# TensorE's eight chunks of a recurrence written out one by one, in place of a loop on registers

## The reference: what is computed

```python
def step(S, inp):
    rt, wt, kt, vt, at, bt = inp
    S = (S * wt[:, :, None, :]
         + jnp.einsum('bhij,bhj->bhi', S, at)[..., None] * bt[:, :, None, :]
         + vt[..., None] * kt[:, :, None, :])
    return S, jnp.einsum('bhij,bhj->bhi', S, rt)
S_fin, y = lax.scan(step, S0, (r, w, k, v, -kk, kk * a))
```

## Time and profile before

| what | value |
|---|---|
| three runs | 4151.55, 4153.0, 4154.53 us; median 4153.0 |
| profiled execution | 4150.38 us, its span 4148.7 us |
| mean granted TensorE clock in the span | 0.941 of full speed |
| TensorE busy with matmuls | 3701.4 us (89%) |
| VectorE, ScalarE, GpSimd busy | 1607.5, 958.5, 53.6 us |
| moved by DMA | 496.8 MB, 119 GB/s from and to HBM over the span |

### The profile page before, as it was taken

How to read it: one execution, slowest core, us unless ns; L and a number is a source line. 1 busy time by engine, 2 the same in 40 slices (tenths; PEclk the granted TensorE clock), 3 DMA queues, 4 the chain that set the end, 5 groups by cost and what they waited for, 6 DMA issues and landing times. The chain is left out here.

```text
span 4148.7 us, 76893 instructions
## 1 busy us (share of the span) xinstructions
PE 3701.4 (89%) x32597; PEld 3463.7 (83%) x32597; DVE 1607.5 (39%) x2336; ACT 958.5 (23%) x1142; POOL 53.6 (1%) x72
## 2 busy tenths in 40 slices
PE   8998997766188987889998699999999999999998
PEld 7998994533188877779995299999999999999997
DVE  3223435502766654332322123333433343344334
ACT  3111112302233333221312113221121112112112
POOL 0000000000001000000000000000000000000000
PEclk9999998966599999999999799999999999999999
DMA  4322228987100004732123622222222222222222
GB/s 156 114 104 92 91 83 351 402 351 287 41 1 0 0 14 152 266 120 91 71 91 132 264 91 71 92 92 92 92 92 91 86 93 89 92 92 92 89 95 72
DMA packets 102399, 496.80 MB, mean 120 GB/s; under 512 B 13121, under 2 KB 19522, under 8 KB 66114
## 3 DMA queue, kind: packets, MB, share of 16 engines
q1 hardware_dynamic: 97538, 476.93, 30.7%
q0 software_dynamic: 4672, 17.01, 1.1%
HBM read 472.32 MB, written 21.58 MB: 119 GB/s over the span
## 5 line engine op out<-in xcount | busy, mean ns | idle before, releaser
L1953 PE MATMUL ps<-hf_hi,whi_f 128*128 128x260 f32 x2816 | 568.3, 283 | 19.3 <-DVE x L1943 9.4
L1953 PE MATMUL ps<-hf_hi,wlo_f 128*128 128x260 f32 x2816 | 567.9, 283 | 0.0
L1953 PE MATMUL ps<-hf_lo,whi_f 128*128 128x260 f32 x2816 | 567.0, 283 | 0.0
L184 ACT ACTIVATE whi_f<-raw 128x2048 fp32r<-128x2048 f32 x132 | 252.8, 1915 | 970.2 <-PE ps L1953 947.9
L1953 PEld LDWEIGHTS ps<-hf_hi,whi_f 128*128 128x128 f32 x2816 | 434.8, 189 | 21.2 <-DVE x L1943 10.6
L1953 PEld LDWEIGHTS ps<-hf_hi,wlo_f 128*128 128x128 f32 x2816 | 434.6, 189 | 0.0
L1953 PEld LDWEIGHTS ps<-hf_lo,whi_f 128*128 128x128 f32 x2816 | 433.5, 188 | 0.0
L188 DVE TENSOR_TENSOR wlo_f<-raw,whi_f 128x2048 fp32r<-128x2048 f32 x132 | 302.6, 2293 | 146.9 <-ACT whi_f L184 146.9
L222 PE MATMUL ps<-h_hi,whi_a 128*128 128x260 f32 x1600 | 324.2, 284 | 29.0 <-DVE h_lo L267 17.8
L222 PE MATMUL ps<-h_hi,wlo_a 128*128 128x260 f32 x1600 | 324.0, 284 | 0.0
L222 PE MATMUL ps<-h_lo,whi_a 128*128 128x260 f32 x1600 | 323.6, 284 | 0.0
(11 more groups left out here) (367 smaller groups left out, 5473.2 us busy)
## 6 DMA issues: line engine op xcount, KB each, us to landing
raw<-w SPq DMA_DIRECT2D x262, 1024.0 KB, 4.8
page_ring<-kc SPq DMA_DIRECT2D x128, 512.0 KB, 6.2
page_ring<-vc SPq DMA_DIRECT2D x128, 512.0 KB, 6.1
mem_ring<-mkc SPq DMA_DIRECT2D x8, 2048.0 KB, 17.2
mem_ring<-mvc SPq DMA_DIRECT2D x8, 2048.0 KB, 17.2
qkv<-ev_a POOLq DMA_DIRECT2D x24, 260.0 KB, 2.3
qkv_head<-qkv SPq DMA_DIRECT2D x8, 780.0 KB, 6.8
rkv<-xt SPq DMA_DIRECT2D x4, 1040.0 KB, 8.4
```

Source lines behind the costliest of these rows:

```text
L184: act.activation(whi[:, u, :], raw[:, u, :], ACT.Copy).then_inc(whi_done, 1)
L1953: mm = pe.matmul(ps[:, 2 * u + s, 0:m], wt[:, wslot, kcol:kcol + 128], t[:, k, a:a + m], start=(first and wt is whi and t is th), stop=(la ...
```

## The change

TensorE no longer uses `turns_of` in the recurrence. Its body is called eight times with a Python number, so that all eight chunks stand one behind the other in its program and each wait compares with a constant. The products, their order and every other engine's program stay as they are.

```diff
--- before.py
+++ after.py
@@ -1383,7 +1383,8 @@
                         pe.wait_ge(W0.sem, W0.at("u3b"))
                         for q in range(2):
                             grams(q)
-                        turns_of(pe, body)
+                        for c in range(NCH):
+                            body(c, c == NCH - 1)
 
                 wkv_out = sem("wkv_out")
                 with nc.Block() as block:
```

## The result

The changed kernel takes 4175.4 us (median of five runs, 4173.95 to 4178.98) against 4153.0 us, a ratio of 1.0057 with a 95% interval from 1.0042 to 1.0071: slower by 22 us. The forecast was 4187 us, slower. The profiled execution took 4178.98 us, its span 4177.3 us, 28.6 over the span before; so the profile shown here is of a run at the slow end of the five, and the differences read from it are a little larger than that of the medians.

The account below looks back on a forecast made before the run. The prediction took TensorE to bound the kernel, busy 3701 of 4148.7 us. Eight feed-forward returns at 2.7 + 1.7 us, less 1 us, gave +34 us on 4153.0: 4187 us, own range 4159 to 4205, overall range 4148 to 4203.

Parts of the forecast that it names:

- The recurrence, waits and return: In the recurrence, constant waits and no loop return on TensorE: -1 us together, between 0 and -2.1.
- The 21 blocks more: Unrolled recurrence: its 21 extra instruction blocks are fetched ahead in straight code and cost nothing.
- The shift, 148 instructions: Feed-forward loop: 5524 added instructions, 21 x 256 + 148, move its target 148 toward its block's end.
- The place: Feed-forward loop's target: 157 instructions left in its block before, give or take 5, and 9 after.
- The second pause: After each feed-forward return TensorE waits for a second block: 2.7 us extra idle, 1.0 to 3.1.
- The clock: After each feed-forward return TensorE's clock may fall to half rate: 1.7 us lost, between nothing and 3.4.
- The sum: Eight feed-forward returns at 2.7 + 1.7 us make 35 us, less 1 us: +34 us, from +6 to +52.
- (1): Rival: the feed-forward loop's target isn't near its block's end, so no second miss: 4152 us, chance 0.30.
- (2): Rival: the recurrence's six returns each load their target as the feed-forward's do; unrolling saves 9 us: 4144, chance 0.02.
- (3): Rival: small shifts change which recurrence chunks fall where in the clock's pattern, faster or slower: 4147 to 4157, chance 0.09.
- (4): Rival: the recurrence's straight code isn't fetched in time, 1 us at each of 21 blocks: 4174 us, chance 0.03.

Follow-up runs that it names:

- runs 5: TensorE's eleven feed-forward turns written out in place of their loop, on the kernel before (4132.9 us) and on the changed kernel (4132.7 us).
- N = 160: The kernel before with 160 unused semaphore increments on TensorE's queue in the sample's step, ahead of the feed-forward loop: ratio 1.0086.
- N = 176: The kernel before with 176 unused semaphore increments on TensorE's queue in the sample's step, ahead of the feed-forward loop: ratio 1.0003.
- run 1: The changed kernel with 108 unused semaphore increments on TensorE's queue, restoring the feed-forward loop's place in its block: 4155.2 us, ratio 1.0009.
- run 3: The kernel before with 256 unused semaphore increments, one whole block, on TensorE's queue in the sample's step: 4150.5 us, ratio 0.9996.
- N = 148: The kernel before with 148 unused semaphore increments on TensorE's queue, moving the feed-forward loop as the change does: 4178.3 us, ratio 1.0062.
- N = 132: The kernel before with 132 unused semaphore increments on TensorE's queue in the sample's step, ahead of the feed-forward loop: ratio 1.0017.

## Why the prediction was right

- **The recurrence, waits and return: -1 us, between 0 and -2.1.** Right within what can be seen. The list of waits kept its four rows, and runs 5 put the change's own worth at 0 us (4132.7 against 4132.9), with an uncertainty of some 6 us on either. So -1 us can't be told from nothing.
- **The 21 blocks more at nothing.** Right: no "issue" in the recurrence, and in runs 5 more than 70 blocks at the full pace of matmuls without a pause.
- **The shift, 148 instructions.** Right: 148 increments on the kernel before gave the changed kernel's turns to 0.1 us, 108 on the changed kernel undid them.
- **The place: 157 left before, 9 after.** Off by 11, outside my 5. The matmuls that ran, nine where I had three or four, show 168 and 20. The step that failed is the distance between sequencer and array. I took the 20 records that were to come when the *target's* packet started, and used them for a packet asked for at a block's entry. A branch spends more time ahead of its packet. The window of the kernel before from the branch to the start of the packet, the stretch ahead of the earlier trace rows:

```profile
2994.10:2995.04 0.94, 0.94 (x10) 0.94 (x10) 0.08 (x1) 0.00 (x0) 0.00 (x0) 1.00 0.00 0
```

  So 40 records were to come at the branch and 20 when its packet started. If a packet at a block's entry starts 0.7 us behind its request, as it does behind the return, only 11 records pass, the sequencer is 29 ahead, and 137 + 29 + 2 = 168. This was worked out after the fact and not tested by itself.
- **The second pause: 2.7 us a return, 1.0 to 3.1.** Measured 1.6 to 2.0, 1.8 in the mean. The time until the block comes was right (2.9 to 3.3 us from restart to restart, where I had 3.2); what was mis-sized is the work in hand, 1.3 us for nine matmuls and not 0.4.
- **The clock: 1.7 us a return.** Near: a stretch of 3.4 us at 0.50 at each return, of which some 0.45 us still fall in the pause in the return shown, so that matmuls lose 1.5 us; this is what the second pause of 1.8 leaves of the 3.3 us by which a turn grew. That the clock would fall was argued, from a pause longer than 1.5 us; the size was only the middle of two bounds, and its coming out is luck.
- **The sum.** 8 x 3.3 = 26 us in the profiled execution, 22 in the medians, against 34. Nearly all of the difference lies in the place: N = 160, with 8 instructions left where I had thought of 9, comes to 4.5 us a return and 37 us in the medians, where I had 4.4 and 35.
- **The rivals.** (1) is what happens with N = 176. It was farther than I thought: not ten instructions but more than 20 were needed to carry the target across. (2) is false for the recurrence and true for the feed-forward loop, as runs 5 show. The Trainium skill's rule ("Runtime: NRT & Kernel Launch", "Instruction fetch mechanics"), that a taken branch to code not held waits for a fetch and that kernels should therefore be unrolled where they can, holds for the feed-forward loop, where writing out gained 18 us; for the recurrence, whose returns took 0.21 us, it gained nothing. (3) stays open in size, though the runs show that it exists: the recurrence took 366.3 to 366.8 us in six of the ten profiled executions and 362.8 to 363.4 in four (run 1, run 3, N = 176 and the last of 5), and chunks of 45 and 47 us follow each other differently. Loops and written-out chunks are in both groups, so it isn't the change's. The eleven executions of run 1 spread from 4146.8 to 4159.1 us. Whether this makes its 1.0009 nothing shows. (4) is refuted: there is no "issue" in the recurrence.

## What to carry to other kernels

The time of a loop on the chip whose return fetches its target again (here a body of over nine blocks; that of the recurrence, under four, didn't) depends on where its first instruction lies, and any edit ahead of it in the engine's program moves that. So a change of half a per cent in a stage that the edit doesn't touch is to be sought there: look for pauses marked "issue" a few instructions behind a return, and shift the code by a few cheap instructions before believing in the edit's own worth. Such a loop on the engine that bounds the stage is worth writing out, 18 us here; the loop whose returns fetched nothing cost nothing that could be measured.

## What the hardware showed that I had not expected

- With 20 instructions left in the target's block a return costs 3.3 us more than with 168, with 8 left 4.5 us, and with the target past the boundary nothing.
- A block boundary a few instructions ahead of the branch can make the branch itself slower: 3.96 us in the median and up to 4.83, against 3.48 and 3.86. It did so in the five returns of eight in which the next block's packet was sent ahead of the target's.
- First pauses of 1.4 to 1.9 us alone left the clock at 1.00, in the kernel before and in all returns of runs 1, 3 and N = 176. With nine matmuls between them, two pauses of 1.3 to 2.0 us brought it to 0.50 in 15 of 16 returns (changed kernel and N = 148); two of 1.55 us did not. With N = 132 a single pause of 2.39 us and one of 3.06 did, while 2.30 and 2.54 us, followed by 17 matmuls and a second pause of 0.5 and 1.0, did not.
